# A second block as one order of work or as two interleaved programs

## The reference, cut to what matters

```python
def swiglu(x, w13, w2):
    a, b = split(x @ w13, 2)
    return (silu(a) * b) @ w2
def ffn_half_step(h, g, shift, scale, gate, w13, w2):
    return h + 0.5 * gate * swiglu(rms_norm(h, g) * (1 + scale) + shift, w13, w2)

m, mc = nine modulation vectors of 1024 each: silu(c) @ w_ada[i] + b_ada[i], and for c_ctx
h, hc = ffn_half_step(h, ..w13_ffn1[i]..), ffn_half_step(hc, ..same weights..)   # d_ff 2816
z, zc = modulated norms @ w_in[i]                       # 1376 columns
k, v  = keys and values of z; kc, vc of zc (in the last layer zc has these columns alone)
h  = h + m[5] * (mix_heads(z, [k, kc], [v, vc]) @ w_out[i])
h  = ffn_half_step(h, ..w13_ffn2[i]..)
if i == 0:
    hc = hc + mc[5] * (mix_heads(zc, kc, vc) @ w_out[i])
    hc = ffn_half_step(hc, ..w13_ffn2[i]..)
# at the end: rms_norm(h, g_final)
```

## Time and profile before

| | |
|---|---|
| median of 3 runs | 4035.07 us (4033.82 to 4037.08) |
| profiled execution: its time as a run | 4036.63 us |
| its span, first to last instruction | 4034.6 us |
| mean granted clock of TensorE | 0.946 |
| HBM read | 340.55 MB |
| weight blocks split (L2108) | 440 |

### The profile page before, as it was taken

How to read it: one execution, slowest core, us unless ns; L and a number is a source line. 1 busy time by engine, 2 the same in 40 slices (tenths; PEclk the granted TensorE clock), 3 DMA queues, 4 the chain that set the end, 5 groups by cost and what they waited for, 6 DMA issues and landing times. The chain is left out here.

```text
span 4034.6 us, 47247 instructions
## 1 busy us (share of the span) xinstructions
PE 3673.1 (91%) x19008; PEld 2966.7 (74%) x19008; DVE 2287.4 (57%) x5186; ACT 1058.9 (26%) x1633; POOL 216.9 (5%) x189
## 2 busy tenths in 40 slices
PE   5899998999889999977889999998999997789997
PEld 3755886788778888765547888887888885457886
DVE  5564556755666666755355666676666535434334
ACT  2354002322331111233242212123112123233222
POOL 1012101000010000100100000010000011000000
PEclk9998887999989999988989999998999998899999
DMA  5532003344323333333102333332333313012332
GB/s 160 152 97 72 1 1 86 112 119 119 104 65 97 105 103 107 91 96 95 46 16 84 95 105 94 110 100 79 95 110 96 97 49 88 27 42 84 94 94 68
DMA packets 663803, 348.33 MB, mean 86 GB/s; under 512 B 29989, under 2 KB 658919, under 8 KB 663328
## 3 DMA queue, kind: packets, MB, share of 16 engines
q1 hardware_dynamic: 662432, 342.69, 30.3%
q10 hardware_dynamic: 1152, 2.62, 0.2%
HBM read 340.55 MB, written 4.72 MB: 86 GB/s over the span
## 5 line engine op out<-in xcount | busy, mean ns | idle before, releaser
L1733 PE MATMUL psum<-hn_high,high 128*128 128x512 f32 (+2 forms) x3360 | 1231.1, 366 | 114.3 <-DVE hn_low L2139 62.3
L1735 PE MATMUL psum<-hn_high,low 128*128 128x512 f32 (+2 forms) x3360 | 1204.3, 358 | 0.0
L1734 PE MATMUL psum<-hn_low,high 128*128 128x512 f32 (+2 forms) x3360 | 1200.6, 357 | 0.0
L1733 PEld LDWEIGHTS psum<-hn_high,high 128*128 128x128 f32 (+1 forms) x3360 | 639.6, 190 | 245.0 <-DVE hn_low L2139 85.5
L1735 PEld LDWEIGHTS psum<-hn_high,low 128*128 128x128 f32 (+1 forms) x3360 | 639.0, 190 | 102.8 <-issue 1.2
L1734 PEld LDWEIGHTS psum<-hn_low,high 128*128 128x128 f32 (+1 forms) x3360 | 640.8, 191 | 93.1 <-issue 1.5
L2108 DVE TENSOR_TENSOR low<-stage,high 128x1024 fp32r<-128x1024 f32 (+3 forms) x440 | 523.9, 1210 | 186.0 <-ACT high L1439 185.4
L2164 DVE SCALAR_TENSOR_TENSOR partial<-stage,cond,partial 128x128 f32<-128x128 f32 x2304 | 625.1, 346 | 0.0
L1439 ACT ACTIVATE high<-stage 128x1024 fp32r<-128x1024 f32 (+3 forms) x440 | 437.0, 1016 | 504.8 <-DMA stage<-in_w_ffn 364.8
L1733 PE MATMUL psum<-hidden_high,high 128*128 128x512 f32 (+1 forms) x1408 | 502.1, 357 | 3.9 <-DVE low L2108 3.9
L1735 PE MATMUL psum<-hidden_high,low 128*128 128x512 f32 (+1 forms) x1408 | 494.1, 351 | 0.0
(11 more groups left out here) (304 smaller groups left out, 3145.0 us busy)
## 6 DMA issues: line engine op xcount, KB each, us to landing
stage<-in_w_ffn SPq DMA_DIRECT2D x240, 512.0 KB, 4.4
stage<-in_w_ada SPq DMA_DIRECT2D x192, 512.0 KB, 4.0
stage<-in_w_in SPq DMA_DIRECT2D x56, 512.0 KB, 5.2
stage<-in_w_out SPq DMA_DIRECT2D x32, 512.0 KB, 4.2
stage<-in_w_ffn SPq DMA_DIRECT2D x32, 384.0 KB, 3.9
stage<-in_w_gate SPq DMA_DIRECT2D x22, 512.0 KB, 3.9
stage<-in_w_up SPq DMA_DIRECT2D x22, 512.0 KB, 5.1
stage<-in_w_down SPq DMA_DIRECT2D x16, 512.0 KB, 4.2
```

The source lines that it names most:

```text
L1733: self.e.matmul(out, high[:, i], xh, start=first and i == 0, stop=False)
L1734: self.e.matmul(out, high[:, i], xl, start=False, stop=False)
L1735: done = self.e.matmul(out, low[:, i], xh, start=False, stop=last and i == nk - 1)
```

## The change

- `second_block` becomes two generators, `lead_stream` (main part) and `side_stream` (context). `together` runs them at build time: each `yield` gives a number of microseconds for which the program has nothing to issue; `self.now` advances by `cost` of what is issued. A program that has waited comes first, then the side while `side.urgent` (up to the end of its mixer of layer 0), else the lead. The lead waits for "side mixed" ahead of its first mixer and for the side's keys ahead of each attention; the side's keys of layer 1 wait for the main attention of layer 0.
- Half steps are no longer shared; each part asks for the weights itself. The side has groups of 4 or 3 hidden tiles (with 4, a down block holds two column tiles), the main part's first half step groups of 6 and 5. Main sums are issued in two halves with a `yield` between. A part has two of the four `banks`, the side has four temporaries of its own.
- `weights` brings the second split block ahead. Stages and slots may skip one that is taken.
- Modulation jobs are also taken in z, in down tiles of a main part alone (every second or fourth), in the main w_out, and at every second hidden tile of the side. Number and content are unchanged.
- Silu of the gate is one ScalarE function, issued behind the gate sum; the VectorE product with the gate sum goes. Gelu and the first block's silu keep the sigmoid.
- SBUF is laid out anew so that the side's half steps and the main mixers stand beside each other. Token-Fourier tables and the raw gating weights come through the stages. The main attention uses two pairs of banks for scores and two single banks for the rest.

```diff
+GROUPS_BESIDE = ((0, 6), (6, 6), (12, 5), (17, 5))
+GROUPS_SIDE = ((0, 4), (4, 4), (8, 4), (12, 4), (16, 3), (19, 3))
...
-            later = [m for m in range(n + 1, min(n + 4, len(plan))) if plan[m][5]]
-            target = later[0] if later else n
+            later = [m for m in range(n + 1, min(n + 5, len(plan))) if plan[m][5]]
+            target = later[1] if len(later) > 1 else later[0] if later else n
...
+    def together(self, lead, side):
+        ready, waited = {lead: self.now, side: self.now}, {lead: False, side: False}
+        while ready:
+            streams = [x for x in ((side, lead) if self.side.urgent else (lead, side)) if x in ready]
+            due = sorted((x for x in streams if ready[x] <= self.now), key=lambda x: not waited[x])
+            stream = due[0] if due else min(streams, key=ready.get)
+            self.now = max(self.now, ready[stream])
+            gap = next(stream, None)
+            if gap is None:
+                del ready[stream]
+            else:
+                ready[stream], waited[stream] = self.now + gap, gap > 0
...
     def modulated_norm(self, name, part, gain, shift, after):
...
+        yield 4.0 + T / 128
         for k in range(KT + 2):
...
+            if k < KT + 1:
+                yield T / 450
...
+    def swiglu(self, name, part, groups, hidden, w_a, a0, w_b, b0, w_down, gate, meanwhile=None):
+        T = part.T
+        halves = ((0, KT // 2), (KT // 2, KT)) if part is self.main else ((0, KT),)
+        for first, tiles in groups:
+            wide = tiles == 4
+            for f in range(tiles):
+                at = first + f
+                key = name, at
+                n, slot, view = self.weights(w_a, 0, KT, a0 + at * P)
+                bank_a = part.banks.next()
+                self.open_sum(bank_a)
+                for lo, hi in halves:
+                    if lo:
+                        yield 0
+                    self.cost(3 * (hi - lo) * T / 2200)
+                    self.products(("gate_sum", key, hi), ...)
+                slot.free = [("gate_sum", key, KT)]
+                yield 0
+                n, slot, view = self.weights(w_b, 0, KT, b0 + at * P)
+                if at and (part is self.main or at % 2):
+                    self.pump_background()
+                t = part.temps.next()
+                s = t.ap[:, 0:T]
+                self.gate_tile(key, bank_a.ap[:, 0:T], t, s)
...
+                self.up_tile(key, bank_b.ap[:, 0:T], s, hidden[0][:, f, :], hidden[1][:, f, :], part.hidden_free)
+                yield 0
...
+            yield max(0.0, 3.0 - 0.7 * (tiles - 1))
+            for f in range(KT):
+                if not wide or f % 2 == 0:
+                    n, slot, view = self.weights(w_down, first * P, tiles, f * P, cols=2 * P if wide else P)
...
+                if part is self.main and f % (4 if wide or tiles < 8 else 2) == 1:
+                    self.pump_background()
+                if f % 2 or part is self.main:
+                    yield 0
...
     def attention(self, m, part, all_q):
...
-                if qt == (2 if m.nt > 2 else 0):
-                    self.pump()
+                if jobs and qt == (2 if m.nt > 2 else 0):
+                    jobs.pop(0)()
+                yield 1.5
...
+    def lead_stream(self):
+        main, hidden = self.main, self.mem.hidden
+        yield from self.plain_norm(main, "final", True)
+        for layer in range(2):
+            yield from self.half_step(main, layer, "g_ffn1", 0, *((GROUPS, hidden["whole"]) if layer else
+                                                                  (GROUPS_BESIDE, hidden["beside"])))
+            while layer == 0 and "side mixed" not in self.events:
+                yield 3.0
+            yield from self.mixers(main, layer, False)
...
+            yield from self.half_step(main, layer, "g_ffn2", 6, GROUPS, hidden["whole"])
+
+    def side_stream(self):
+        side, hidden = self.side, self.mem.hidden["side"]
+        side.urgent = True
+        yield from self.half_step(side, 0, "g_ffn1", 0, GROUPS_SIDE, hidden, normed=True)
+        yield from self.mixers(side, 0, False)
+        side.urgent = False
+        self.events |= {"side mixed", ("kv", 0)}
...
+        yield from self.half_step(side, 0, "g_ffn2", 6, GROUPS_SIDE, hidden)
+        yield from self.half_step(side, 1, "g_ffn1", 0, GROUPS_SIDE, hidden)
+        while ("attention", (0, "main")) not in self.events:
+            yield 3.0
+        yield from self.mixers(side, 1, True)
+        self.events.add(("kv", 1))
...
-    def gated_tile(self, key, ps_a, ps_b, t, s, high, low, hidden_free):
-        self.wait_ge("gate_sum", key)
+    def gate_tile(self, key, ps, t, s):
+        self.wait_ge("gate_sum", key, KT)
         self.wait_free(t)
-        self.e.activation(s, ps_a, ACT.Sigmoid).then_inc(*self.mark("gate_sigmoid", key))
+        self.e.activation(s, ps, ACT.Silu).then_inc(*self.mark("gated", key))
...
-        self.e.tensor_tensor(s, s, ps_a, ALU.mult).then_inc(*self.mark("gated", key))
         self.wait_ge("gated", key)
```

More of the change, by code:

```diff
@@ L392, in __init__ @@
         self.side = Part("ctx", CTX, mem.h_ctx, mem.mean_ctx, 1)
+        self.main.banks, self.main.temps = self.banks, self.temps
+        self.side.temps = Turn([Spot(mem.side_tmp[:, i, :]) for i in range(4)], skip=True)
+        self.now, self.events = 0.0, set()
     def mark(self, *key):
@@ L502, in pieces, with cost, linear @@
         return stage, views
-    def linear(self, name, w, n_k, c0, width, parts, take, tile=P, background=True, middle=False):
+    def cost(self, us):
+        self.now += us
+    def linear(self, name, w, n_k, c0, width, part, ready, take, x=None, tile=P, background=True, middle=False):
+        T, x = part.T, x or part.hn
         for at in range(0, width, tile):
             cols, f = min(tile, width - at), at // tile
-            held = {}
             for k in range(0, n_k, KT):
@@ L799, in take_v @@
             self.jobs.append(turn)
[L800 removed]
+        self.whole(self.linear("v", w, KT, 1024, 512, main, main.hn_ready, take_v))
         self.flush()
@@ L961, in norm_for_half_step, with half_step, half_gate @@
                    self.mod_ready)
-        self.modulated_norm(name, part, mem.gain[:, :, part.col:part.col + 1], rows(first, part.col), [("gain", name)])
-    def half_step(self, parts, layer, names, first):
-        half = {}
-        def half_gate(part):
-            if part.name not in half:
+        yield from self.modulated_norm(name, part, mem.gain[:, :, part.col:part.col + 1], rows(first, part.col), [("gain", name)])
+    def half_step(self, part, layer, names, first, groups, hidden, normed=False):
+        half = []
+        def half_gate():
+            if not half:
@@ L974, in half_gate @@
                 part.h_ready = [*part.h_ready, ("half_gate", name)]
-            return half[part.name]
+            return half[0]
         inp = self.mem.inp
         w13, w2 = inp[f"w13_{names[2:]}_2"][layer], inp[f"w2_{names[2:]}_2"][layer]
-        self.swiglu(f"{names}{layer}", parts, w13, 0, w13, D_FF, w2, half_gate)
-    def swiglu(self, name, parts, w_a, a0, w_b, b0, w_down, gate, meanwhile=None):
-        hidden, hidden_free = [self.mem.hidden[part.name] for part in parts], self.hidden_free
-        for first, tiles in GROUPS:
+        if not normed:
+            yield from self.norm_for_half_step(part, layer, names, first)
@@ new lines, in swiglu @@
+                bank = part.banks.next()
+                key = name, first, f
+                cols = slice(P * (f % 2), P * (f % 2 + 1)) if wide else slice(0, P)
+                self.open_sum(bank)
+                self.cost(3 * tiles * T / 2200)
+                self.products(("down_sum", key), bank.ap[:, 0:T], n, [v[:, :, cols] for v in view], hidden, 0, [],
+                              each=[("hidden", (name, first + x)) for x in range(tiles)] if f == 0 else None)
+                if not wide or f % 2:
+                    slot.free = [("down_sum", key)]
```

640 lines of the change are left out of this document (351 added, 289 removed).

## The result

| | before | after |
|---|---|---|
| median of the runs, us | 4034.78 | 4467.35 |
| range of the runs, us | 4033.82 to 4037.08 | 4465.27 to 4473.64 |
| span of the profiled execution, us | 4034.6 | 4463.4 |
| ratio | | 1.107, interval 1.106 to 1.109 |

I forecast 3820 with a range up to 3940. It is 4467: the sign is wrong, and the loss (433 us) is beyond the slower rival's 4085 as well.

A forecast was written before the change was run, and what follows sets the result against it. TensorE, busy 91% of the span, was taken as the bound wherever its queue is full. Gains 14 (A) + 57 + 70 + 23 + 72 = 236, less 5 (DMA) and 13, gave 218 off 4034.6: 3817, said as 3820, range 3740 to 3940.

The forecast's parts named there:

- Two blocks ahead: Weight prefetch: a split gets 2.7 us more, so side blocks are priced at 2.7; taken as 0, bounds -10 and +16.
- the first block moves by over 15 us: Sign set down in advance: if the first block moves by that much, the prediction is wrong.
- Splits and DMA: Second reading of weights: VectorE's 250 us of extra splits hidden while parts mix, DMA barely fits; 5 us lost, bounds 0 and 20.
- A: Side's ffn1 alone, right behind block one: VectorE decides, 215 us taken against 229 before, gain 14.
- fill terms: Slack of TensorE filled by interleaving the two programs in C, D, F and H: 57, 70, 23 and 72 us.
- C: Side mixer of layer 0, filled by main's ffn1: 57 of 67 us of slack gained.
- D: Main mixer of layer 0 to the next half step, filled by side steps: 70 of 92 us of slack gained.
- F: Norms before the next half step, ahead of layer 1's mixers: 23 of 26 us of slack gained.
- H: Mixers of layer 1: slack 104 us, 27 of it left open in attention and last norm, 72 gained.
- None has to be forced in a burst: Modulation vectors: 69 done at the second block's start where 56 are needed, 80 at side's mixer where 80 are; net 0.
- rival 2: In-order queues with guessed gaps or table reloads halve the fill in the second block: 125 us less, 3910; chance 0.25.
- Rival 3: VectorE becomes the bound where both parts are in half steps, extra splits paid in full: 4085 us, slower; chance 0.08.

The follow-up runs named there:

- e1: The changed kernel with one weight block brought ahead instead of two, the programs still interleaved: 4257.8 us, ratio 1.055.
- e4: e1 with the two programs run one after the other, giving way only when one must wait for the other: 4229.8 us.
- e13: e1 plus e9's depth rule, e10's cut of side's low halves and e12's dropped vectors, interleaved: 4101.1 us.
- e14: The same three changes as e13, with the two programs one after the other: 4154.7 us.
- e5: The kernel before with only the three shared half steps parted, main's then side's, each reading its own weights: 4309.4 us, ratio 1.068.
- e9: e1 with two blocks ahead only where the next four blocks of the plan are all split: 4212.8 us.
- e10: e1 with only the first 128 of 1024 low-half columns computed for blocks side's half steps read, interleaved: 4166.5 us.
- e12: e1 where side's gate and up tiles no longer start a modulation vector: 4238.2 us.
- e6: The kernel before with two blocks ahead only where the next four blocks of the plan are all split: 3985.5 us, ratio 0.988.
- e8: e1 without the modulation vectors added between z tiles and in the first block's down products: 4288.4 us.

## Why the prediction was wrong, step by step

**The step that failed first: "Two blocks ahead ... Taken as 0, bounds -10 and +16".** It measured +210 in the changed kernel and +284 in the old one. I had counted what a second block ahead gives a late split (it does: the earlier trace rows show such splits, and mending them gave 46 us in the mixers), and not what it takes: a transfer in flight holds one of four stages, and its split is issued ahead of work that frees the stage. The rows for it stood in the profile: the SP queue's waits for `partial` and `mod`, and the first block, where DMA issue follows the end of the sums by 0.03 us. The prediction never used them. One of its signs did catch it: "the first block moves by over 15 us" was to show it wrong; it moved by 237.

**Second, "Splits and DMA ... hidden as long as steps of the two parts mix", 5 us.** The second reading costs 273 us alone in the old kernel. Of it in the changed kernel, at one ahead, I can show 91 us as VectorE's part of side's splits and 20 as the vectors between them. Pricing VectorE by its sum (65%, from the durations of the earlier trace rows) was the error: what counts is the turn of each block, and a side block leaves 2.7 us for a chain of transfer, two splits and perhaps 4.2 us of sums. So A, "215", became 284 us in after (295 in e1, 260 light).

**Third, the fill terms, 57 + 70 + 23 + 72.** The net of interleaving, against the same kernel apart, is -28 us and not 222. The residuals of the profiled executions split it. Up to the end of side's mixer and of main's ffn1, e1 takes 857 us (1133 to 1990) and e4 815 (1132 to 1947): 42 lost, where C was to gain 57. From there to the last residual it is 2242 against 2249: 7 gained, where D, F and H were to gain 165. In e13 and e14 the same two parts are 832 against 765 (67 lost) and 2106 against 2232 (126 gained). So the filling of D, F and H exists, once blocks come in time; with late blocks it is nearly gone. In main's mixer (1989 to 2453 in e1) TensorE waits 47.8 us for low halves, 21.5 in the old mixer: side's blocks are late in the very gaps they should fill, and ScalarE and VectorE do main's chain and side's splits in one order. That is rival 2's mechanism, and its 3910 had the size wrong: "half back" was more than all back.

**Fourth, "None has to be forced in a burst".** The prediction counted the vectors up to the side's mixer and not for what comes next: the norm of the side's ffn2 wants 96 of the 176, while main is still in its first half step. In all interleaved kernels `have_vectors` makes the missing ones in one go there, 7 in after and e1, 15 in e13. VectorE does nothing else, and TensorE nearly stands. First e1, then e13:

```profile
1667.00:1694.00 27.00, 7.76 (x30) 7.15 (x31) 25.99 (x106) 2.11 (x2) 0.00 (x0) 0.51 0.42 121
```

```profile
1615.00:1676.00 61.00, 16.58 (x64) 15.10 (x65) 59.99 (x241) 2.11 (x2) 0.00 (x0) 0.50 0.44 127
```

TensorE is idle for 19 of 27 and 44 of 61 us. None of the kernels run apart has such a stretch, so it is part of the 42 and the 67 us, and e1 is 28 us behind e4 with 19 of idle time in it. No run tried it by itself.

**Rival 3** (4085) named splits paid in full, 250 us, and said VectorE would become the bound. It is at 58% in e1. The price was of that size (273 us in e5), the mechanism was waiting and not work, so the match is luck.

**What held:** silu 0; transfers 451.63 MB, 103 more (forecast 106); splits 676 for 440, 236 more (228); no filler in layer 1's attention; ScalarE's table loads 64 for 32, of 1283 ns each as in the earlier trace rows (I had allowed 60 in all). What these loads cost within chains was not tried by itself in the interleaved kernel. The Trainium skill's about 2.7 us in the prediction ("ScalarE: Activation LUTs", What ACT_TABLE_LOAD costs) is a load of 1283 ns and the drain behind it: the trace agrees with the load, and shows no drain as a row of its own.

**What stays open.** Of the 223 us that remain at one ahead, 156 are accounted for by e9, e10 and e12 (of these, 45 are a gain that the old kernel could have too, and has in e6). 30 are the first block's vectors, which cost more still when they are made later (e8). 19 are idle time in the burst, and in e13, which is 64 us behind the kernel before, 44 are. Two more places show in e4, where nothing is interleaved. Main's mixer of layer 0 takes 325 us against 285; its w_out, into which the change puts eight vectors, takes 58 of them instead of 38, and the SP queue waits 51.5 us there for `mod`. Main's ffn1 of layer 0 takes 435 us against 409 in e5, while in layer 1, with the old groups, it is 396 and 395. The prediction had 13 us for all smaller items and 0 for the vectors' places. The causes within these two, guessed turns and fewer banks a part were not tried by themselves.

## What to carry to other kernels

Before a prefetch is deepened, follow one buffer round: who frees it, what stands in that engine's queue ahead of the freeing, and whether that waits for the transfer itself. The time of one turn, divided by the tiles it carries, must stay below the tile's time; a change that leaves less work behind a block needs the same check as one that doubles the depth. Work that is made on the way must be counted up to every place that demands it, the next one included. Read the waits of the queue that issues transfers even where its engine shows no busy time, and cost a block by its turn, not an engine by its sum.

## What the runs showed of the hardware

- TensorE's granted clock follows its holes: in 120 to 420 us it was 0.92 with 279.44 us busy before, and 0.82 with 221.74 us busy after, in the same part of the program. In the 27 us of e1's burst, with 7.76 us busy, it was 0.51, which is nearly all at the lower of the two levels, 1.2 and 2.4 GHz. Over whole kernels with the same 19008 matmuls, busy time is 3673 us at a clock of 0.946, 3721 at 0.940 (e4), 3754 at 0.936 (e1), 3810 at 0.919 (after): kernels that stall more also take longer for the same matmuls.
- A transfer of 512 KB landed 3.8 to 6.5 us after its issue (medians 3.9 and 5.2, for the modulation and the projection blocks) in 120 to 420 us of after, where the DMA engines had room (share 0.29); in the circle the 6.15 us from issue to the split are the largest term.
- Matmuls of 256 columns follow each other at a median of 0.118 us, also where nothing waits; I had read 0.114 from a short stretch. Times 4752 of them in side's half steps, that is 19 us.
